# Four waits of GpSimd's weight splits for a normed input's rests, and block 2's sums rounded row by row, in a two-block fp32 kernel

## What is computed

```python
# block 1, each layer
h_l = _rmsnorm(x, g_pre[l]) * (1.0 + sc_l) + sh_l
pl = _split_proj(h_l @ w_in[l])
...
# block 2
h = rms_norm(x, norm_mix[layer])
proj = h @ w_in[layer]
...
y = jnp.einsum('nbsm,nmd->bsnd', branches, w_branch[layer])
gate = jax.nn.sigmoid(mg.reshape(B, S, N_BRANCH, D_MODEL).astype(jnp.float32)).astype(y.dtype)
x = x + jnp.sum(gate * y, axis=2) @ w_out[layer]
h = rms_norm(x, norm_mlp[layer])
x = x + jnp.square(jax.nn.relu(h @ w_up[layer])) @ w_down[layer]
```

## Time and profile before

| what | value |
|---|---|
| median of 3 runs | 4196.48 us (4193.07 to 4197.07) |
| the profiled execution's own time | 4197.54 us |
| its span, first to last instruction | 4195.7 us |
| mean granted TensorE clock | 0.955 of full speed |
| busy: PE, DVE, ACT, POOL | 3878.6, 1880.7, 974.4, 1959.9 us |
| POOL's L867 and L869 | 415 passes each, mean 2358 and 2371 ns |

### The profile page before, as it was taken

The page is one execution under the profiler, slowest core; times in us unless marked ns, Lnnn a source line. Parts: engine busy times, 40 slices in busy tenths (PEclk is TensorE's granted clock), DMA queues, the critical chain, the costliest instruction groups (busy, mean ns, idle before and its releaser), DMA issues. The chain is left out here.

```text
span 4195.7 us, 52077 instructions
## 1 busy us (share of the span) xinstructions
PE 3878.6 (92%) x19691; PEld 3083.5 (73%) x19691; DVE 1880.7 (45%) x2716; ACT 974.4 (23%) x1729; POOL 1959.9 (47%) x834
## 2 busy tenths in 40 slices
PE   5999999999989989899999998898898998999999
PEld 4777788888877877576678777676585454877877
DVE  5344326656638882344425655355304555133200
ACT  3333212222210011333312222101214444112200
POOL 2333342332326554244454343687452210887886
PEclk7999999999999999899999999999898998999999
DMA  7211221121225543222222121334422110443433
GB/s 191 49 47 43 74 56 46 44 48 41 52 76 112 117 110 101 60 56 58 75 66 56 44 61 48 90 90 119 128 57 56 38 31 14 95 105 78 96 91 90
DMA packets 481706, 305.17 MB, mean 73 GB/s; under 512 B 37786, under 2 KB 451875, under 8 KB 480635
## 3 DMA queue, kind: packets, MB, share of 16 engines
q1 hardware_dynamic: 469434, 282.43, 28.0%
q10 hardware_dynamic: 12096, 20.33, 1.4%
HBM read 276.42 MB, written 26.27 MB: 72 GB/s over the span
## 5 line engine op out<-in xcount | busy, mean ns | idle before, releaser
L867 POOL TENSOR_TENSOR whi<-ring,con 128x1024 fp32r<-128x1024 f32 (+1 forms) x415 | 978.6, 2358 | 2180.6 <-DMA ring<-in_w_in 1681.4
L551 PE MATMUL ps<-xT_parts,whi 128*128 128x512 f32 (+2 forms) x2632 | 1007.1, 383 | 77.0 <-DVE hT_parts L2099 37.7
L551 PE MATMUL ps<-hT_parts,whi 128*128 128x512 f32 (+1 forms) x2864 | 1049.2, 366 | 0.0
L869 POOL TENSOR_TENSOR ring_parts<-ring,whi 128x1024 fp32r<-128x1024 f32 (+1 forms) x415 | 983.9, 2371 | 32.5
L551 PE MATMUL ps<-xT_parts,ring_parts 128*128 128x512 f32 (+2 forms) x2600 | 944.3, 363 | 0.0
L551 PE MATMUL ps<-arena_parts,whi 128*128 128x512 f32 (+1 forms) x2472 | 765.9, 383 | 74.2 <-DVE arena_parts L2093 63.2
L1551 ACT ACTIVATE arena<-ps 128x512 f32<-128x512 f32 (+7 forms) x583 | 311.5, 544 | 1671.2 <-PE ps L551 960.3
L551 PE MATMUL ps<-arena 128*128 128x128 f32 (+9 forms) x3292 | 647.7, 341 | 27.8 <-DVE arena L2061 22.1
L551 PEld LDWEIGHTS ps<-xT_parts,whi 128*128 128x128 f32 (+1 forms) x2632 | 500.3, 190 | 182.7 <-issue 64.3
L551 PEld LDWEIGHTS ps<-hT_parts,whi 128*128 128x128 f32 x2864 | 544.1, 190 | 91.1 <-issue 7.2
L551 PEld LDWEIGHTS ps<-arena_parts,whi 128*128 128x128 f32 x2472 | 460.0, 194 | 181.4 <-issue 73.9
(11 more groups left out here) (160 smaller groups left out, 3377.1 us busy)
## 6 DMA issues: line engine op xcount, KB each, us to landing
ring<-in_w_in SPq DMA_DIRECT2D x504, 256.0 KB, 4.0
arena<-in_w_ada SPq DMA_DIRECT2D x80, 256.0 KB, 6.2
ring<-in_w_up SPq DMA_DIRECT2D x64, 256.0 KB, 4.0
ring<-in_w_down SPq DMA_DIRECT2D x64, 256.0 KB, 3.6
ring<-in_w_out SPq DMA_DIRECT2D x48, 256.0 KB, 3.8
gates_kept<-stage ACTq DMA_DIRECT2D x24, 384.0 KB, 4.0
arena<-gates_kept SPq DMA_DIRECT2D x24, 384.0 KB, 3.7
ring<-in_w_br_attn SPq DMA_DIRECT2D x32, 256.0 KB, 3.9
```

Source lines behind the costliest of these rows:

```text
L551: return nc.tensor.matmul(o, l, r, start=first, stop=last)
L867: v.tensor_tensor(hi, raw, ones[:, 0:m].unsqueeze(1).to_broadcast([P, kt, m]), ALU.mult).then_inc(w_rounded, 1)
L869: v.tensor_tensor(ringR[:, s, 0:kt, 0:m], raw, hi.bitcast(F32), ALU.subtract).then_inc(w_split, 1)
```

## The change

POOL's stream gets four waits on `h_lo`, each for all 8 rests of a normed input. In layer 0 it stands ahead of the third tile of the stage, in layer 1, block 2 and the MLP ahead of the fourth. The number and the order of the splits stay. Some of them stand written out where a loop of four was. In block 2, the third branch's loop is written out on ACT and DVE; ACT rounds row f-1 behind the tanh of row f, into the place of block 2's constants (`acc2P`) rather than into the arena's `roundA`; DVE makes the rest of row f-1 behind the sum of row f. The barrier is gone, and `bring_x` waits for PE's release of the last branch tile instead.

```diff
@@ names @@
+        acc2P = parts(con[:, C_AT["cos"][0]:C_AT["cos"][0] + KT * LAT].rearrange("p (f n) -> p f n", f=KT), acc)
@@ SP @@
-                sp.wait_ge(phase, 3 * phases_to(before))
+                if before:
+                    sp.wait_ge(phase, 3 * phases_to(before))
+                else:
+                    sp.wait_ge(w_used, used)
...
-                    bring_x("branches2", LAT, 3)
+                    bring_x(None, LAT, 3, tiles.number() - 4)
@@ POOL @@
-                split_all(28 + 8)
+                    split()
+                    split()
+                else:
+                    for _ in range(3):
+                        split()
+
+                pool.wait_ge(h_lo, KT * (l + 1))
+                for _ in range(2 - l):
+                    split()
+                split_all(24 + 8)
...
-            split()
-            split()
-
-            for _ in range(10):
+            for _ in range(3):
+                split()
+
+            pool.wait_ge(h_lo, 3 * KT)
+            for _ in range(9):
                 split()
...
-            split_all(8 + 32 + 32)
+            split_all(8)
+            for _ in range(3):
+                split()
+
+            pool.wait_ge(h_lo, 4 * KT)
+            split()
+            split_all(28 + 32)
@@ PE @@
-            if phase_end("branches2"):
-                return
-            summed_tiles(accP, LAT)
+            summed_tiles(acc2P, LAT)
@@ ACT @@
+            def gate2():
+
+                p = product()
+                last_read()
+                release(do(tha2, bank(2 * p), ACT.Tanh, scale=0.5))
+                skip()
+
+            def round_row2(f):
+
+                act.wait_ge(acc_row, f + 1)
+                do(acc2P[0][:, f], acc[:, f, 0:LAT], ACT.Copy).then_inc(part_hi, 1)
+
-            for b in range(3):
+            for b in range(2):
...
-            if phase_end("branches2"):
-                return
-            round_rows(accP, acc, LAT)
+            for f in range(KT):
+                gate2()
+                if f:
+                    round_row2(f - 1)
+            round_row2(KT - 1)
@@ DVE @@
-            for b in range(3):
+            for b in range(2):
...
-            if phase_end("branches2"):
-                return
+            def row_rest2(f):
+
+                dve.wait_ge(part_hi, acc2_from + f + 1)
+                v.tensor_tensor(acc2P[1][:, f, 0:LAT], acc[:, f, 0:LAT], acc2P[0][:, f].bitcast(F32),
+                                ALU.subtract).then_inc(part_lo, 1)
+
+            for f in range(KT):
+                skip()
+                p = product()
+                last_read()
+                own.settle()
+                dve.wait_ge(acc_row, f)
+                release(stt(tmp2, tha2, 1.0, bank(2 * p), ALU.add, ALU.mult))
+                last_read()
+                dst = acc[:, f, 0:LAT]
+                stt(dst, tmp2, 0.5, dst, ALU.mult, ALU.add).then_inc(acc_row, 1)
+                if f:
+                    row_rest2(f - 1)
+            row_rest2(KT - 1)
...
-            keep_rest(accP, acc, LAT)
```

More of the change, by code:

```diff
@@ L74 @@
                              for p in ("attn", "branch1_", "gla", "branch2_", "conv", "branch0_")] \
-    + ["kv2", "cmp", "heads", "branches2", "up", "down", "end"]
+    + ["kv2", "cmp", "heads", "up", "down", "end"]
 def phases_to(name):
@@ L499, in two_blocks @@
         fill_kept, gates_turned = sem("fill_kept"), sem("gates_turned")
+        acc_row = sem("acc_row")
         u_hi, u_square = sem("u_hi"), sem("u_square")
@@ L679, in keep_x, with bring_x @@
                     sp.dma_start(x_dram[:, 4 * h:4 * h + 4, 0:n], xT[:, 4 * h:4 * h + 4, 0:n]).then_inc(x_kept[h], 16)
-            def bring_x(before, n, kept):
-                sp.wait_ge(phase, 3 * phases_to(before))
+            def bring_x(before, n, kept, used=None):
+                if before:
+                    sp.wait_ge(phase, 3 * phases_to(before))
+                else:
+                    sp.wait_ge(w_used, used)
                 for h in range(2):
@@ L2669, in _ @@
                             own(stt(dst, tmp2, 0.5, dst, ALU.mult, ALU.add))
-            if phase_end("branches2"):
-                return
+            acc2_from = parts_made[0]
+            parts_made[0] += KT
+            def row_rest2(f):
[15 more added lines that the diff above has]
+            row_rest2(KT - 1)
             def residual():
```

## The result

Five runs of each kernel, side by side: 4196.48 us before, **4174.71 us** with the change (4172.58 to 4178.60), a ratio of 0.9950 with a 95% interval from 0.9937 to 0.9963. The profiled execution took 4177.55 us, its span is 4175.7, 20.0 less than the 4195.7 of before.

A forecast was written before the change was run, and what follows sets the result against it. PE, busy 92% of the span, was taken as the bound, so only its waits and clock matter. 3.8 + 4.1 + 4.1 + 10.5 - 2.0 = 20.5 us off 4197.54 gave 4177.0, or 4176.0 for the median; range 4168 to 4186.

The forecast's parts named there:

- Layer 1, 3.8 taken: Layer 1's normed input: without the fourth split's collisions, last rest and PE's first tile end 3.8 us earlier, 2.8 to 4.8.
- Layer 0, +2.0 taken, 0 to 2.5: Layer 0's normed input: the wait brings nothing; evenly spaced rows keep PE's clock low, costing 2.0 us, 0 to 2.5.
- Block 2's input and the MLP's, 4.1 each: Residuals ahead of both norms lose their split collisions: 4.1 us each, block 2 3.1 to 5.1, MLP 2.9 to 4.1.
- The rival by which block 2's gain stops at ACT: Block 2's input: ACT's DMA chain, if set by traffic, loses the 4.1 us; 4180 us, chance 0.07.
- The sums, 10.5 taken, 7.9 to 15.1: Block 2's sums: PE starts rows without idling, first w_out tile ends sooner; 10.5 us taken, 7.9 to 15.1.
- the middle case, 11.8: Block 2's sums: POOL is early by part of a pass, row 7's rest is there at 3757.5, gaining 11.8 us.
- the low end's mechanism: Block 2's sums: PE's clock falls in idle times of 1 to 3 us, costing up to 2.5; 7.9 us gained.
- The ideal of 15.1: Block 2's sums: with no collision at all the first w_out tile takes 5.6 us, gaining 15.1 us.
- The step that failed: Block 2's sums: x returns from DRAM some 4 us earlier and is not late for the first product.
- POOL as the pace of the third branch: Rival, block 2's third branch: DVE's sums and rests hold POOL beyond its idle time; 4180 or 4186 us, chance 0.08.
- The slower rival: Layers 0 and 1: held splits collide with key and query norms, 5.9 us slower than before, 4202 us; chance 0.03.

The follow-up runs named there:

- the experiment with one wait: Kernel before plus one POOL wait: block 2's third and fourth w_out_2 tiles split behind the sums' last rest, barrier kept; 4186.00 us, ratio 0.9977.

## Why the prediction was right, step by step

- **Layer 1, 3.8 taken**: B fell by 4.2, in the range of 2.8 to 4.8. The mechanism gave what was taken: the last rest came 3.8 us sooner after the first scaling, 18.2 in place of 22.0. The extra is the clock, and luck: the matmuls of 256 columns were at 0.28 from 4.0 us after row 7's start, not 5.0 as in the earlier trace rows, and over the kernels with this wait B lies anywhere between 24.25 and 25.85.
- **Layer 0, +2.0 taken, 0 to 2.5**: 1.1 in the profile, 1.1 to 1.9 over the four profiles with the wait. Mechanism and sign were shown by taking the wait out.
- **Block 2's input and the MLP's, 4.1 each**: 4.2 and 4.1. The rival by which block 2's gain stops at ACT is out, since C ends behind PE's wait for ACT.
- **The sums, 10.5 taken, 7.9 to 15.1**: the second w_out tile began 11.85 us earlier against the last branch product. That is the middle case, 11.8, with POOL early by part of a pass; PE's clock didn't fall in idle times of 0.85 and 1.80 us, and that was luck in part: in two of the four other profiles with the same sums it fell behind 1.15 and 1.80 us, the low end's mechanism, and cost some 1.3 us of the 2.5 allowed for it. Over those four D fell by 9.7 to 10.9 us. The ideal of 15.1 was out of reach because the rests of rows 6 and 7 collided, 5.66 us for the two. The split into 7.7 for the collisions and the rest for the barrier comes from the experiment with one wait.
- **The step that failed**, with no term of the sum on it: "x returns from DRAM some 4 us earlier, and is not late for the first product." It came back later than the product: DVE waited 5.45 us for it. Against DVE's pass over the last branch product x was issued 2.3 us earlier than before (1.4 us behind it, 3.7 before), but the first w_out product was ready over 11 us earlier. Of the 11.85 us, 0.8 was given back by the last residual, so D fell by 11.0; with the rests faster still, up to 5.8 us hung on x (D 56.61 against 50.83). It was small in this profile, and it became the next bound. The "some 4 us" stood on no row.
- **POOL as the pace of the third branch**: didn't happen, but its idle time of 0.83 us ahead of a gate tile shrank to between 0.32 and 0.64 us, and to nothing in the last pair, as the added rests take what was free.
- **The slower rival**, held splits on the rope chain: the idle time of the earlier trace rows ahead of the first key's rotation was 4.07 us in place of 3.81. The collisions on it are those of before: DVE's longest pass of the next norm takes 2.53 us, before 2.56.

The sum of the terms was 20.5; the stretches sum to 22.5, the medians show 21.8. The surplus is four small misses of the same sign: 0.9 in layer 0, whose cost was taken too high, 0.5 in the sums, 0.4 in layer 1 and 0.1 in block 2.

## What to carry to other kernels

Where two engines exclude each other and one of them has time to spare, make that one wait. It cost nothing here where the consumer of the held work was further off than the work took, and a wait of one line was worth 4 to 8 us in each of eight places (the 8 is block 2's sums with the wait in place of the reordering; on top of the reordering D fell by 2 us more in one profile and rose in two). Cutting POOL's instruction gave little, because DVE had passes queued. Look first whether the stage makes up for the collision anyway (layer 0), since PE's clock may then be better off with it, and ask of each gain what arrives next: here a transfer that no one had waited for before.

## What the runs showed of the hardware

- DVE passes with both operands in SBUF and POOL passes excluded each other instruction by instruction: 3.1 us against whole POOL passes of 2.4, 1.48 against quarters, 0.95 alone. POOL is held too: 2.94 in place of 2.36 us. Cutting changed the grain and not the sum: 4.2 us lost in place of 4.3.
- Short idle times went with a late rise of PE's clock in layer 1's sums: with breaks of 0.39 and 1.12 us among the rows it stayed low for over 10 us, without them it was up 3.3 us after the start. In a stream that had been at the full level, idle times of 0.85 and 1.80 us, with a row's matmuls between them, were followed by no matmul at the lower level. Matmuls at the lower level did follow a pair of 1.15 and 1.80 us (in two profiles) and single ones of 2.21 and 3.15 us; behind one of 2.80 us there were none. So their length alone didn't decide it, and what did stays open.
- One and the same transfer of x, 2 MB, took 9.8 and 13.1 us from its issue to the pass that waited for it, in two executions of one kernel.
